# Down projections of a SwiGLU trunk: four of eleven pairs of k tiles by seven block products in place of eight

## What is computed

```
g, u = split(rmsnorm(x) @ w_in)      # w_in  1024 x 5632
x = x + 0.5 * (silu(g) * u) @ w_out  # w_out 2816 x 1024, the down projection
```

## Time and profile before

| | |
|---|---|
| median of 3 runs | 1103.48 us (1102.86 to 1103.87) |
| the profiled execution, its own time | 1103.8 us |
| its span, first to last instruction | 1101.8 us |
| mean granted clock of TensorE | 0.997 |
| TensorE matmul busy | 1088.5 us, 99% of the span |
| VectorE busy | 724.6 us, 66% |
| ScalarE busy | 543.7 us, 49% |
| GpSimd busy | 394.6 us, 36% |

### The profile page before, as it was taken

One profiled execution on the slowest core, in us unless ns is written; L12 is line 12 of the kernel. 1 busy time (PEld: TensorE's weight loads), 2 busy tenths in 40 slices (PEclk: granted clock), 3 DMA queues, 4 the chain that ended last, 5 costly groups with the idle time before them and its releaser, 6 DMA issues.

```text
span 1101.8 us, 14159 instructions
## 1 busy us (share of the span) xinstructions
PE 1088.5 (99%) x5356; PEld 921.0 (84%) x5356; DVE 724.6 (66%) x848; ACT 543.7 (49%) x608; POOL 394.6 (36%) x775
## 2 busy tenths in 40 slices
PE   8999999999999999999999999999999999999996
PEld 7887888889898888888888888888988988888885
DVE  6665556799776755655665665568997766666552
ACT  6453444754556544443454544357455645444431
POOL 0678632000000057673226858210000003686800
PEclk9999999999999999999999999999999999999998
DMA  8977556653653476765667676555455436677651
GB/s 279 283 228 232 179 191 224 204 178 127 218 192 108 144 227 216 217 214 201 212 208 216 206 234 203 199 196 199 146 178 187 171 125 193 211 215 230 201 192 57
DMA packets 183364, 215.92 MB, mean 196 GB/s; under 512 B 18986, under 2 KB 138358, under 8 KB 183296
## 3 DMA queue, kind: packets, MB, share of 16 engines
q1 hardware_dynamic: 158144, 200.82, 55.2%
q0 software_dynamic: 24064, 13.16, 4.4%
q10 hardware_dynamic: 1088, 1.05, 0.3%
HBM read 200.79 MB, written 1.05 MB: 183 GB/s over the span
## 4 chain that ended last, share of the span: by engine, by line
PE 86%; issue 6%; POOL 3%; DVE 2%; DMA 2%; ACT 1%; DVEq 0%; POOLq 0%; SPq 0%; ACTq 0%
PE acc L1391 24%; PE acc L1393 24%; PE acc L1392 24%; PE acc L1407 3%; PE acc L1409 3%; PE acc L1408 3%; POOL kT L423 3%; PE turn L1287 2%; DMA kT<-kT 1%; DVE w_lo L791 1%; ACT w_hi L461 1%; PE acc L1354 1%; PE acc L1371 0%; PE acc L1360 0%; PE acc L1588 0%
## 5 line engine op out<-in xcount | busy, mean ns | idle before, releaser
L791 DVE TENSOR_TENSOR w_lo<-w_raw,w_hi 128x2048 fp32r<-128x2048 f32 (+1 forms) x190 | 426.7, 2250 | 196.7 <-ACT w_hi L461 196.6
L461 ACT CAST w_hi<-w_raw 128x2048 fp32r<-128x2048 f32 (+1 forms) x190 | 355.3, 1871 | 139.2 <-PE acc L1393 127.1
L423 POOL DMA_DIRECT2D kT<-kT x704 | 344.7, 498 | 164.4 <-DVE kT L923 122.4
L1391 PE MATMUL acc<-w_hi,xT 128*128 128x512 f32 x808 | 316.7, 392 | 0.0
L1393 PE MATMUL acc<-w_hi,xT 128*128 128x512 f32 x808 | 314.7, 389 | 0.0
L1392 PE MATMUL acc<-w_lo,xT 128*128 128x512 f32 x808 | 314.4, 389 | 0.0
L1391 PE MATMUL acc<-w_hi,hT 128*128 128x512 f32 x544 | 213.2, 392 | 0.0
L1393 PE MATMUL acc<-w_hi,hT 128*128 128x512 f32 x544 | 211.9, 389 | 0.0
L1392 PE MATMUL acc<-w_lo,hT 128*128 128x512 f32 x544 | 211.8, 389 | 0.0
L412 POOL TENSOR_TENSOR rstd<-var,mhalf 128x2 f32<-128x2 f32 x14 | 22.4, 1597 | 479.1 <-DVE var L847 332.4
L1393 PEld LDWEIGHTS acc<-w_hi,xT 128*128 128x128 f32 x808 | 151.7, 188 | 31.9
(11 more groups left out here) (148 smaller groups left out, 923.7 us busy)
## 6 DMA issues: line engine op xcount, KB each, us to landing
w_raw<-in_ffn_w_in SPq DMA_DIRECT2D x172, 512.0 KB, 4.8
w_raw<-in_ffn_w_out SPq DMA_DIRECT2D x80, 512.0 KB, 4.4
w_raw<-in_mix_w_in SPq DMA_DIRECT2D x32, 512.0 KB, 4.5
w_raw<-in_xattn_wkv SPq DMA_DIRECT2D x32, 512.0 KB, 4.3
kT<-kT POOLq DMA_DIRECT2D x704, 16.0 KB, 3.3
w_raw<-in_mix_w_out SPq DMA_DIRECT2D x16, 512.0 KB, 4.1
w_raw<-in_xattn_wq SPq DMA_DIRECT2D x16, 512.0 KB, 4.5
w_raw<-in_xattn_wo SPq DMA_DIRECT2D x16, 512.0 KB, 4.2
```

The lines of the kernel that those rows point to most:

```text
L423: pool.dma_start(hfeat[B * q:B * q + B, g % 2, a * RUN:(a + 1) * RUN], hblk[B * a:B * a + B, g % 2, q * RUN:(q + 1) * RUN]).then_inc(hfeat ...
L461: act.copy(w_hi[:, u % SLOTS, 0:n], w_raw[:, u % SLOTS, 0:n]).then_inc(w_split_hi, 1)
L791: dve.tensor_tensor(w_lo[:, u % SLOTS, 0:n], w_raw[:, u % SLOTS, 0:n], w_hi[:, u % SLOTS, 0:n].bitcast(F32), ALU.subtract).then_inc(w_spli ...
L1391: pe.matmul(o, hi, wh, start=(first and i == 0), stop=False)
```

## The change

In a down projection, k tiles are taken in pairs (2p, 2p+1). With the two token tiles as rows, a pair is a 2 x 2 block matrix of the hidden values times a 2 x 2 block matrix of the weights (two k tiles by two column halves). For the pairs p = 0 to 3 its result is now made by the seven products of the Strassen-Winograd form; the other seven pairs stay as they were. This is done in all four down projections.

- **Units.** A down projection has 18 units in place of 12 (`DOWN`); they are called d0 to d17 below. A pair has a `singles` unit (three products: two with plain hidden tiles, one with a token sum; 9 matmuls) and a `sums` unit (four products, 12 matmuls). Two singles/sums couples stand in a row at d4 to d7. d0, d3, d8 and d12 have four k tiles, d11 and d13 to d17 two.
- **Weight sums.** For a pair VectorE makes four sums of weight blocks (128x1024, 128x512, 128x512 in a chain) from the `singles` slot of `w_raw` into the next slot (`weight_sums`). The `sums` unit has no DMA.
- **Token sums.** In chunks 1 to 4 VectorE makes four 128x128 sums of hidden blocks (`token_sums`). In chunk 10 ScalarE casts them (`sum_hi`) and VectorE makes the residues (`sum_lo`), 128x512 each.
- **Adding up.** Four products have PSUM banks of their own, shared by more than one block of the result. `shared_half`, `shares` and `last_shares` add them into x with one ScalarE and eight VectorE operations of 128x512.
- **Order.** d5 is now split ahead of the last hidden cast. `shares` stands after the split of d12, and `last_shares` after `x_blocks`. The split of the unit after the projection (`U_MI`) now stands ahead of `gained_blocks`, on both engines. The same edits are made at the second feed-forward (`U_F2O`).

The core of the diff (SyncE's loop loads `singles` as whole rows of two k tiles, `square_parts`):

```diff
+    SEVEN = 4
+    DOWN = [("rows", 0, 8, 4), ("singles", 0), ("sums", 0), ("rows", 0, 12, 4), ("singles", 1), ("sums", 1), ("singles", 2), ("sums", 2),
+            ("rows", 0, 16, 4), ("singles", 3), ("sums", 3), ("rows", 0, 20, 2), ("rows", 1, 8, 4), ("rows", 1, 12, 2),
+            ("rows", 1, 14, 2), ("rows", 1, 16, 2), ("rows", 1, 18, 2), ("rows", 1, 20, 2)]
+    D_SUMS = [i for i, e in enumerate(DOWN) if e[0] == "sums"]
+    D_LAST = [max(i for i, e in enumerate(DOWN) if e[:2] == ("rows", n)) for n in range(2)]
...
+                    elif e[0] == "singles":
+                        unit(u, at, square_parts(u, src_out, l, 2 * e[1]))
+                    else:
+                        sp.wait_ge(w_split, at.at(UNITS, u + 1))
+                        sp.sem_inc(w_landed[u % SLOTS], 32)
...
+                if e and e[0] == "sums":
+                    act.wait_ge(t_ready, at.at(2 * SEVEN, SEVEN * f + e[1] + 1))
+                else:
+                    act.wait_ge(w_landed[u % SLOTS], at.at(32 * (UNITS // SLOTS), 32 * (u // SLOTS + 1)))
                 act.wait_ge(unit_done, at.at(2 * UNITS, 2 * u + 2))
-                act.copy(w_hi[:, u % SLOTS, 0:n], w_raw[:, u % SLOTS, 0:n]).then_inc(w_split_hi, 1)
+                if e and e[0] == "singles":
+                    act.copy(w_hi[:, u % SLOTS, 0:GN], w_raw[:, u % SLOTS, 0:GN])
+                    act.copy(w_hi[:, u % SLOTS, 2 * GN:n], w_raw[:, u % SLOTS, 2 * GN:n]).then_inc(w_split_hi, 1)
...
+                    if c == FC - 1:
+                        sum_hi(0)
...
+                    if c == FC - 1:
+                        for p in range(1, SEVEN):
+                            sum_hi(p)
...
+                def sum_hi(p):
+                    at = Layer(l)
+                    act.wait_ge(s_sum_ready, at.at(2 * SEVEN, SEVEN * f + p + 1))
+                    act.wait_ge(unit_done, at.at(2 * UNITS, 2 * SLOTS + 2 * (base + 2 * FC - 1) + 2))
+                    act.copy(s_parts[p][:, :, 0, :], s_sum[p].rearrange("p (a s) -> p a s", a=2)).then_inc(s_hi_ready, 1)
...
                 split_hi(base + 2 * FC + 4, Layer(l))
+                split_hi(base + 2 * FC + 5, Layer(l))
                 hidden_hi(FC - 1)
-                state["next"] = base + 2 * FC + 5
+                state["next"] = base + 2 * FC + 6
...
+            def shared_half(f, at):
+
+                u = (U_F1O, U_F2O)[f] + D_SUMS[-1]
+                act.wait_ge(unit_done, at.at(2 * UNITS, 2 * SLOTS + 2 * u + 2))
+                act.wait_ge(s_ready, at.at(2 * SEVEN, SEVEN * f + SEVEN))
+                act.activation(shared, product_banks(f)[1][:, :], ACT.Copy, scale=0.5).then_inc(shared_ready, 1)
...
-                weights_to(U_F1O + 7, at)
+                weights_to(U_F1O + D_LAST[0] + 1, at)
+                shared_half(0, at)
+                weights_to(U_F1O + D_LAST[0] + 2, at)
                 squares(0, 0, at)
-                weights_to(U_F1O + 11, at)
+                weights_to(U_MI, at)
...
+                if e and e[0] == "singles":
+                    weight_sums(u, at)
                 dve.wait_ge(w_split_hi, at.at(UNITS, u + 1))
-                dve.tensor_tensor(w_lo[:, u % SLOTS, 0:n], w_raw[:, u % SLOTS, 0:n],
-                                  w_hi[:, u % SLOTS, 0:n].bitcast(F32), ALU.subtract).then_inc(w_split, 1)
+                if e and e[0] == "singles":
+                    dve.tensor_tensor(w_lo[:, u % SLOTS, 0:GN], w_raw[:, u % SLOTS, 0:GN],
+                                      w_hi[:, u % SLOTS, 0:GN].bitcast(F32), ALU.subtract)
+                    dve.tensor_tensor(w_lo[:, u % SLOTS, 2 * GN:n], w_raw[:, u % SLOTS, 2 * GN:n],
+                                      w_hi[:, u % SLOTS, 2 * GN:n].bitcast(F32), ALU.subtract).then_inc(w_split, 1)
...
+            def weight_sums(u, at):
+
+                w = w_raw[:, u % SLOTS, :].rearrange("p (i j n) -> p i j n", i=2, j=2)
+                s = w_raw[:, (u + 1) % SLOTS, :].rearrange("p (c n) -> p c n", c=4)
+                dve.wait_ge(w_landed[u % SLOTS], at.at(32 * (UNITS // SLOTS), 32 * (u // SLOTS + 1)))
+                dve.wait_ge(w_split, at.at(UNITS, SLOTS + u - 1))
+                steps.link(dve.tensor_tensor(s[:, 0:2, :], w[:, :, 1, :], w[:, 0, :, :], ALU.subtract))
+                steps.link(dve.tensor_tensor(s[:, 2, :], w[:, 1, 1, :], s[:, 0, :], ALU.subtract))
+                dve.tensor_tensor(s[:, 3, :], w[:, 1, 0, :], s[:, 2, :], ALU.subtract).then_inc(t_ready, 1)
...
+                    if c == FC - 1:
+                        sum_lo(0)
                     split_lo(base + 2 * c + 4, at)
...
                         hidden_lo(c - 1)
+                    if c == FC - 1:
+                        for p in range(1, SEVEN):
+                            sum_lo(p)
                     split_lo(base + 2 * c + 5, at)
...
+                    if c < SEVEN:
+                        token_sums(c, hfeat[:, g % 2, :].rearrange("p (a k t s) -> p k t a s", a=NBLK, k=2, t=T))
...
+                def token_sums(p, h):
+                    s = s_sum[p].rearrange("p (i a s) -> p i a s", i=4, a=NBLK)
+                    n = steps.mark(dve.tensor_tensor(s[:, 0, :, :], h[:, 0, 1, :, :], h[:, 1, 1, :, :], ALU.add))
+                    dve.tensor_tensor(s[:, 2, :, :], h[:, 0, 0, :, :], h[:, 0, 1, :, :], ALU.subtract)
+                    steps.wait(n)
+                    steps.link(dve.tensor_tensor(s[:, 1, :, :], s[:, 0, :, :], h[:, 0, 0, :, :], ALU.subtract))
+                    dve.tensor_tensor(s[:, 3, :, :], h[:, 1, 0, :, :], s[:, 1, :, :], ALU.subtract).then_inc(s_sum_ready, 1)
+
+                def sum_lo(p):
+                    dve.wait_ge(s_hi_ready, Layer(l).at(2 * SEVEN, SEVEN * f + p + 1))
+                    dve.tensor_tensor(s_parts[p][:, :, 1, :], s_sum[p].rearrange("p (a s) -> p a s", a=2),
+                                      s_parts[p][:, :, 0, :].bitcast(F32), ALU.subtract).then_inc(s_ready, 1)
+
...
+            def into_x(n, t, src, scalar):
+
+                o = xs[:, t, n * GN:(n + 1) * GN]
+                if scalar is None:
+                    return steps.mark(dve.tensor_tensor(o, src, o, ALU.add))
+                return steps.mark(dve.scalar_tensor_tensor(out=o, in0=src, scalar=scalar, in1=o, op0=ALU.mult, op1=ALU.add))
+
+            def shares(f, at):
+
+                u = (U_F1O, U_F2O)[f] + D_SUMS[-1]
+                m = product_banks(f)
+                dve.wait_ge(unit_done, at.at(2 * UNITS, 2 * SLOTS + 2 * u + 2))
+                dve.wait_ge(shared_ready, at.at(2, f + 1))
+                into_x(0, 0, shared, None)
+                steps.link(dve.scalar_tensor_tensor(out=shared_6, in0=m[6][:, :], scalar=0.5, in1=shared, op0=ALU.mult, op1=ALU.add))
+                steps.link(dve.scalar_tensor_tensor(out=shared, in0=m[7][:, :], scalar=0.5, in1=shared_6, op0=ALU.mult, op1=ALU.add))
+                steps.wait(into_x(0, 1, shared, None))
+
+            def last_shares(f):
+
+                m5 = product_banks(f)[5]
+                n = [into_x(1, 0, shared_6, None), into_x(1, 1, shared, None)]
+                for t in range(T):
+                    steps.wait(n[t])
+                    n[t] = into_x(1, t, m5[:, :], 0.5)
+                steps.wait(n[T - 1])
 
             for l in range(L):
...
-                weights_to(U_F1O + 7, at)
-                update(0, 0, 0, U_F1O + 5, F1O_PAIR[0], 0.5, at)
-                update(0, 0, 1, U_F1O + 5, F1O_PAIR[0], 0.5, at)
+                weights_to(U_F1O + D_LAST[0] + 1, at)
+                shares(0, at)
+                weights_to(U_F1O + D_LAST[0] + 2, at)
+                update(0, 0, 0, U_F1O + D_LAST[0], F1O_PAIR[0], 0.5, at)
+                update(0, 0, 1, U_F1O + D_LAST[0], F1O_PAIR[0], 0.5, at)
                 for t in range(T):
                     x_blocks(2 * l, t)
-                weights_to(U_F1O + 11, at)
+                last_shares(0)
+                weights_to(U_MI, at)
                 gained_blocks(2 * l, G_MIX)
                 xT_lo_part(1, 0, 0, at)
                 xT_lo_part(1, 0, 1, at)
-                weights_to(U_MI, at)
-                update(0, 1, 0, U_F1O + 11, F1O_PAIR[1], 0.5, at)
+                update(0, 1, 0, U_F1O + D_LAST[1], F1O_PAIR[1], 0.5, at)
                 weights_to(U_MI + 1, at)
-                update(0, 1, 1, U_F1O + 11, F1O_PAIR[1], 0.5, at)
+                update(0, 1, 1, U_F1O + D_LAST[1], F1O_PAIR[1], 0.5, at)
                 gained(1, 1, 0, G_MIX, "mi10", at, l)
                 xT_lo_part(1, 1, 0, at)
...
+                def singles(u, p):
+
+                    first, last = p == 0, p == SEVEN - 1
+                    pe.wait_ge(w_split, at0.at(UNITS, SLOTS + u + 1))
+                    if first:
+                        pe.wait_ge(hact_ready, at0.at(4 * FC, T + 2 * FC * f + 2 * FC))
+                        if (l, f) == (0, 0):
+                            pe.wait_ge(memT_ready, 4)
```

(13 more changed lines are left out.)

99 lines of the change are left out of this document (71 added, 28 removed).

## The result

The changed kernel takes 1146.61 us (median of 4 runs, 1145.30 to 1147.37), the kernel before took 1103.56 beside it; ratio 1.0391, interval [1.0377, 1.0404]. The predicted direction holds, the size does not: +43 us where I had +22.7, and 1146.6 lies outside the 1113 to 1134 that I had given. So the change costs twice what I had added up.

The account below looks back on a forecast made before the run. TensorE was taken to bound the kernel, VectorE to become the bound. Waits less saved matmuls gave +9.9, +5.3, +5.7 and +1.8 us for the four projections, +22.7 in all, 1126 us; range 1113 to 1134.

Parts of the forecast that it names:

- Prices and matmuls: Down projections: 12 fewer matmuls each, 2.72 us less; strided weight sums priced 1.23, 0.68, 0.68 us; VectorE rises to 59 us.
- it has become the bound: Down projections: VectorE rises from 34 to 59 us, above TensorE's 57.2, and with three slots cannot work ahead.
- Steps 1 and 2: Units d0 to d7, second projection: TensorE waits 2.1 us for d3, 1.6 for d6 and 0.5 for d7.
- The walk: Unit-by-unit timing of VectorE and TensorE through the second down projection: 8.0 us of waits less 2.7, +5.3.
- Step 4: Second half of the projection: d14's residue follows updates, transposes and `last_shares` on VectorE; TensorE waits 1.5 us.
- Step 5: Projection's end: next unit's cast needs d15 done, then a 7.6 us chain against 5.4 of TensorE; opening transpose waits 2.3.
- T: Start of the down projection walked, in us: 494.35 in the second, 136.05 in the first.
- First projection: First down projection: waits 4.8 us at d1, 0.5 d3, 3.0 d6, then 0.5, 1.5, 2.3; 12.6 less 2.7, +9.9.
- if the waits are for DMA: Sign of being wrong: TensorE's waits in the new profile would be for DMA, not VectorE's residues.
- The clock: Sum keeps 2.4 GHz; rival (0.10): after first projection's 4.8 us wait, d1 and d2 run at half speed, 1130.3 us.
- tail covered: Rival (0.14): projection ends cost nothing in the first three projections, 11.4 us less, 1115.
- VectorE keeps up: Rival (0.09): splits come early enough, residue d3 by T + 10.1 instead of 12.2; the saving stands, 1092.6.

Follow-up runs that it names:

- e5: Changed kernel with the second half's four-tile unit last instead of first (two, two, two, two, two, four): 1140.7 us, ratio 1.0339 to the kernel before.
- e6: Changed kernel without GpSimd's shuffle of the next stage's operand, stale values multiplied: 1141.99 us, ratio 1.0350 to the kernel before.
- e14: Changed kernel, SyncE asks for the next stage's second unit only when its first has landed: 1146.67 us, ratio 1.0389 to the kernel before.
- e16: Changed kernel without the next operand's shuffle and with the next stage's second unit held until the first landed: 1141.37 us, ratio 1.0347.
- e1: Changed kernel with `last_shares` moved behind the residue of d15: 1143.38 us, ratio 1.0365 to the kernel before.
- e2: Changed kernel with gains and token residues again ahead of the split of the next stage's first unit: 1148.56 us, ratio 1.0415.
- e4: Changed kernel with `last_shares` behind d15's residue, and gains and first token tile's update ahead of the next unit's split: 1143.97 us, ratio 1.0371.
- e7: Changed kernel with the four pairs spread between units of rows, second half two, two, two, four, four: 1132.74 us, ratio 1.0258.
- e12: Changed kernel with casts and residues of token sums 1 to 3 behind the split of d3: 1145.96 us, ratio 1.0387.

## Why the prediction was right in direction and short in size

- **Prices and matmuls: right.** 48 matmuls fewer. The sum of two strided weight tensors, which had no row, took 1.22, 0.69 and 0.69 us, as assumed; VectorE 57.3 us a projection against 59. But "it has become the bound" was too strong: VectorE idles for 13 to 15 us of the three longer stretches, where I had said below 10.
- **Steps 1 and 2, waits at d3 and d6: d3 right** (2.3, 2.3 and 2.1 for 2.1 in the second to fourth, 0.2 for 0.5 in the first). **d6 near by luck in the second projection** (1.2 for 1.6), low in the third, where it waited 2.6. The walk had the last hidden residue without a wait; VectorE waited for its cast, which the shuffle held:

```profile
526.79 0.69 DVE L1033 TENSOR_TENSOR hT<-kT,hT 128x512 fp32r<-128x512 f32 x1 [1.51 <-ACT hT L569]
```

  In the second projection the slow matmuls behind d3 used up the same 1.4 us, so it didn't show at d6: two errors against each other. The variants bear this out. Where six to eight slow matmuls followed the wait at d3 of the second or third projection (after, e5, e6, e14, e16), d6 waited 1.5 us or less; where none did and the weight sums stood as here (after, e1, e2, e4, e6), 2.0 to 3.0. A dropped clock in front of a queue that is late anyway costs less than its matmuls do.
- **Step 4, d14: right** (1.5 for 1.5), and e1 took it away. d12 waits 0.2 besides, behind d11 of two tiles.
- **Step 5, the opening transpose: this is the step that failed.** "Its cast needs d15 done" was not what held it: d15 was done, the weights weren't there. The step has no term for the landing. The only landing that I had, 4.4 us under "DMA", would just have hidden it: by my walk d15's residue frees the slot at T + 53.0, and 4.4 later is 57.4, the time at which d15 is done. The unit took 8.6 to 9.1 us. Two things were wrong with the 4.4. It is the median of a single DMA, and a unit is two; and it is no reading of this unit, which took 6.6 to 7.0 us in the kernel before, beside the shuffle. That is 2.2 to 2.6 us a projection which the old trace could have told me; the other 1.5 to 2.5 came with the change, and why stays open. The 4.2 us and more between 4.4 and the measured landing explain how 2.3 became 6.0 to 6.6, three times: 11.8 us of the missing 19.4. I had checked transfers ahead of d9, not at this unit, though its slot comes free only when d15 is split and just two two-tile units, 5.4 us, are left to hide it. One of my signs of being wrong was "if the waits are for DMA": the profile names VectorE at the transpose, but the transfer stands behind it.
- **First projection: right in sum** (+10.7 for +9.9) **by two errors against each other.** d1 waited 1.9, not 4.8, since the late hidden residue came 2.3 us ahead of the start (132.27) instead of 0.1; and d6 waited 1.4, not 3.0: the shuffle of chunk 10 began earlier too, and its cast came 2.7 us behind its last issue (at 153.40), not 4.0. This varies between kernels that have the same instructions up to there: in e7 and e12 d1 waited 4.2 and 4.3 for `memT`, near the forecast. The end, 6.2 for 2.3, took it back.
- **The clock: wrongly kept out of the sum, and wrongly placed in the rival.** I gave it one place, d1. There 1.9 us did nothing. It fell elsewhere: d3 of the second, and after all three transposes. Together with slower restarts that is most of the 5.7 us after the transposes and 1.4 in the second projection, some 7 of the missing 19.4 (what is left is small terms of both signs). It follows the waits: most of it stands behind the 6 us at the transposes.
- The rivals "tail covered" and "VectorE keeps up" are out: d3 was ready at T + 12.6.

## What to carry to other kernels

Where one engine prepares blocks for another through a ring of few slots, a saving on the second is worth only what the first can deliver in that place: walk it unit by unit, and put the costly blocks where several cheap, large ones are already prepared; the same two pairs were worth +11 or -3 us by place alone. Small units shorten the time that hides the next transfer, so put them early in a stage and the large ones at its end. A median landing time of single transfers is not the landing of a unit made of several, nor that of the unit in question: read it at that very unit in the old trace (7.0 us here, not 4.4), to the last of its transfers, and add what the new order will put beside it.

## What the runs showed that I had not expected

- **How TensorE's clock falls.** In the 18 profiles with the change or a variant of it, behind the first 125 us, I took every wait of TensorE and looked for a run of matmuls 0.43 us apart (three or more) behind it. Of 49 waits of 0.9 us to under 1.5 none had one, of 43 of 1.5 to 2.1 us 9, of 41 of 2.1 to 3.3 us 25, of 30 above 3.5 us all (in e4, three times, only behind the second wait that follows the transposes). The same wait of 2.28 us did it in one projection of the changed kernel and not in the next. So for waits of 2 to 3 us it can't be foretold from their length; the price was mostly 5 to 9 slow matmuls, 1.0 to 1.8 us, and 13 twice. The rule of the Trainium skill that the prediction names (page "TensorE: Matmul & The Clock Gate", section "Why this matters for your kernels"), that idle gaps bring the slow clock back, agrees with these rows.
- **Holding transfers back gained nothing.** With the second unit held (e14) the transfer engines ran nearly dry while the first was still not there. Windows of that profile (the last two columns are DMA share and GB/s):

```profile
568.00:570.00 2.00, 2.00 (x11) 1.65 (x10) 0.32 (x1) 0.00 (x0) 0.00 (x0) 1.00 0.88 282
570.00:572.00 2.00, 2.00 (x11) 1.65 (x10) 0.00 (x0) 0.00 (x0) 0.00 (x0) 1.00 0.17 56
```

  In the changed kernel the same stretch of its unit ran at 335 to 339 GB/s, and its unit was no later. The cast of e14's unit began at 572.27, behind 2 us in which the engines were busy for 17%: the rate says little of when a unit is complete.
